# The diagonal 16x16 blocks of a delta-rule inverse, solved by forward substitution before the chunk loop instead of by doubling levels inside it

## What is computed

```
lower = where(strict, einsum('bhncd,bhnsd->bhncs', k_beta, k) * decay, 0.0)
sol = triangular_solve(lower, rhs, left_side=True, lower=True, unit_diagonal=True)
...
def step(state, inp):
    v_new = u_i - w_i @ state
    o_i = q_i @ state + a_i @ v_new
    state = state * cd_i + k_i^T @ v_new
```

## Time and profile before

| | |
|---|---|
| median of three runs | 1436.24 us |
| the profiled execution | 1442.7 us, of it 1441.0 us span |
| PE busy | 94% of the span |
| DVE, POOL, ACT busy | 53%, 51%, 38% |
| last projection round ends on PE | 402 us |
| first cum of the chunk stage (step 0) | 409.12 us |
| cum of step 1, of step 2 | 428.18, 456.75 us |
| step 8 begins on PE | 614.41 us |
| first matmul of the output projection | 648.90 us |

### The profile page before, as it was taken

One profiled execution on the slowest core, in us unless ns is written; L12 is line 12 of the kernel. 1 busy time (PEld: TensorE's weight loads), 2 busy tenths in 40 slices (PEclk: granted clock), 3 DMA queues, 4 the chain that ended last, 5 costly groups with the idle time before them and its releaser, 6 DMA issues.

```text
span 1441.0 us, 18144 instructions
## 1 busy us (share of the span) xinstructions
PE 1354.2 (94%) x6707; PEld 1134.1 (79%) x6707; DVE 769.5 (53%) x955; ACT 552.4 (38%) x749; POOL 731.1 (51%) x492
## 2 busy tenths in 40 slices
PE   3799999999968999989987999999999999999997
PEld 3468888888858999877865888888888887888886
DVE  2835344262446666625474656555655556457544
ACT  3234535262541221216264444444444444324321
POOL 4447758685742212222048665656565567444540
PEclk8699999999978999989998999999999999999999
DMA  8142424234250000110111333223333337543601
GB/s 328 41 132 60 131 73 116 74 86 123 66 131 2 1 0 0 58 59 0 30 30 29 89 88 82 70 74 82 88 88 88 88 113 283 181 137 119 232 32 59
DMA packets 137929, 128.42 MB, mean 89 GB/s; under 512 B 7423, under 2 KB 114188, under 8 KB 137868
## 3 DMA queue, kind: packets, MB, share of 16 engines
q1 hardware_dynamic: 137868, 127.60, 29.3%
HBM read 111.85 MB, written 15.74 MB: 89 GB/s over the span
## 4 chain that ended last, share of the span: by engine, by line
PE 69%; POOL 11%; issue 9%; DVE 6%; DMA 3%; ACT 1%; SPq 0%; POOLq 0%; DVEq 0%; ACTq 0%
PE ps L1957 18%; PE ps L1958 18%; PE ps L1959 18%; PE ps L2087 5%; POOL ada_raw L820 3%; PE ps L2106 3%; PE ps L2103 3%; POOL ada_raw L823 2%; POOL w_split L795 2%; DMA ada_first<-in_ada_w_dram 1%; POOL ada_raw L825 1%; DVE ada_first L1468 1%; POOL h_p L919 1%; DVE pm_b L1612 1%; DMA x_hi<-in_x_dram 1%
## 5 line engine op out<-in xcount | busy, mean ns | idle before, releaser
L1957 PE MATMUL ps<-h_p,w_units 128*128 128x512 f32 x616 | 241.9, 393 | 11.5 <-POOL h_p L919 10.0
L1958 PE MATMUL ps<-h_p,w_units 128*128 128x512 f32 x616 | 241.3, 392 | 0.0
L1959 PE MATMUL ps<-h_p,w_units 128*128 128x512 f32 x616 | 241.1, 391 | 0.0
L1957 PE MATMUL ps<-h,w_split 128*128 128x512 f32 x448 | 175.1, 391 | 0.0
L1959 PE MATMUL ps<-h,w_split 128*128 128x512 f32 x448 | 174.3, 389 | 0.0
L1958 PE MATMUL ps<-h,w_split 128*128 128x512 f32 x448 | 174.3, 389 | 0.0
L930 POOL TENSOR_TENSOR w_units<-f_units,w_units 128x512 fp32r<-128x512 f32 x88 | 112.8, 1292 | 113.9 <-ACT w_units L1283 47.6
L955 POOL TENSOR_TENSOR wd_split<-wd_raw,wd_split 128x1024 fp32r<-128x1024 f32 x44 | 109.7, 2500 | 109.5 <-ACT wd_split L1379 109.4
L1957 PEld LDWEIGHTS ps<-h_p,w_units 128*128 128x128 f32 x616 | 116.5, 189 | 37.0 <-issue 8.3
L1908 DVE TENSOR_TENSOR ad_split<-ad_raw,ad_split 128x512 fp32r<-128x512 f32 x40 | 98.5, 2477 | 78.3 <-ACT ad_split L1380 78.3
L1957 PE MATMUL ps<-wd_split,ad_split 128*128 128x512 f32 x352 | 137.1, 390 | 1.6 <-DVE ps L1866 1.3
(11 more groups left out here) (293 smaller groups left out, 2593.4 us busy)
## 6 DMA issues: line engine op xcount, KB each, us to landing
w_up_raw<-in_w_up_dram SPq DMA_DIRECT2D x44, 512.0 KB, 5.2
wd_raw<-in_w_down_dram SPq DMA_DIRECT2D x44, 512.0 KB, 4.2
ada_raw<-in_ada_w_dram SPq DMA_DIRECT2D x32, 512.0 KB, 4.1
w_raw<-in_w_in_dram SPq DMA_DIRECT2D x28, 512.0 KB, 5.4
act_dram<-cg SPq DMA_DIRECT2D x22, 512.0 KB, 3.3
ad_raw<-act_dram SPq DMA_DIRECT2D x44, 256.0 KB, 4.5
ada_first<-in_ada_w_dram SPq DMA_DIRECT2D x4, 2048.0 KB, 17.4
h_room<-in_w_out_dram SPq DMA_DIRECT2D x8, 512.0 KB, 13.4
```

What stands on the lines that cost most here:

```text
L1957: pe.matmul(dst, a_hi, b_hi, start=(first and n == 0), stop=False, skip_group_check=onto)
L1958: pe.matmul(dst, a_hi, b_lo, start=False, stop=False, skip_group_check=onto)
L1959: mm = pe.matmul(dst, a_lo, b_hi, start=False, stop=(last and n == len(pairs) - 1), skip_group_check=onto)
```

## The change

The inverses of all 16x16 diagonal blocks (4 heads x 8 chunks x 8 blocks = 256 blocks) are made once, before the chunk loop. A block lies in one partition, two blocks per partition (`kk_lanes`, `lower_lanes`, `inv_lanes`: 128 partitions x 2 x 16 x 16), and DVE runs forward substitution over the 15 columns, two small operations each. To get there, in the last projection round: PE makes the key products of all chunks between the two halves of the Z tile, ACT copies them to SBUF, SP moves the diagonal blocks to DRAM (32 DMAs) and back in the lane layout, and the gates go the same way (`gate_grid`, `gate_lanes`). The finished inverses go to DRAM and back as rows (`inv_rows`), first chunk 0 alone, then the other seven; `spread` on DVE multiplies them with a block mask into `um`. Levels 0 to 3 go out of the chunk stage: `level_a` is gone, `level_b` does levels 4, 5 and 6 only, and t1 transposes the spread `um`. POOL builds four masks instead of seven. Step 0 on DVE comes after the substitution in its list, and the loop's last projection round is written out separately.

```diff
-        A_LEVELS = [1]
-        B_LEVELS = list(range(2, LEVELS))
+        B_LEVELS = list(range(int(math.log2(SUB)), LEVELS))     # (beside level_mask)
@@ sync @@
+            sp.wait_ge(s.lane_step, L_TAKEN)
+            sp.dma_start(grid_dram.rearrange("a r n -> r a n"), gate_grid[0:NH * TT, :, :]).then_inc(s.diag_moved, 16)
+            sp.wait_ge(s.diag_moved, M_GRID)
+            sp.dma_start(gate_lanes[:, :, :, :], grid_dram.rearrange("a (m r) (b i) -> (r b) a m i", m=2, i=SUB)
+                         ).then_inc(s.diag_moved, 16)
+            sp.wait_ge(s.lane_step, L_DIFF)
+            for index, hd in enumerate(KK_ORDER):
+                sp.wait_ge(s.kk_copied, index + 1)
+                for b in range(NB):
+                    sp.dma_start(kk_dram[hd, :, b, :, :].rearrange("n r c -> r n c"),
+                                 kk_rows[hd][b * SUB:(b + 1) * SUB, :, b * SUB:(b + 1) * SUB]
+                                 ).then_inc(s.diag_moved, 16)
+            sp.wait_ge(s.diag_moved, M_KK_OUT)
+            sp.wait_ge(s.w_lo_done, NH * NPOS)
+            sp.dma_start(kk_lanes[:, :, :, :].rearrange("p m r c -> p m (r c)"),
+                         kk_dram.rearrange("(m h) n b r c -> (h n b) m (r c)", m=2)).then_inc(s.diag_moved, 16)
+            sp.wait_ge(s.lane_step, L_DONE)
+            sp.dma_start(inv_dram.rearrange("(m h) n b r c -> (h n b) m (r c)", m=2),
+                         inv_lanes[:, :, :, :].rearrange("p m r c -> p m (r c)")).then_inc(s.diag_moved, 16)
+            sp.wait_ge(s.diag_moved, M_INV_OUT)
+            inv_v = inv_dram.rearrange("h n b c i -> (b c) h n i")
+            sp.dma_start(inv_rows[:, :, 0, :], inv_v[:, :, 0, :]).then_inc(s.diag_moved, 16)
+            sp.wait_ge(s.diag_moved, M_INV_FIRST)
+            sp.wait_ge(s.dn_um, 1)
+            for hd in range(NH):
+                sp.dma_start(inv_rows[:, hd, 1:TT, :], inv_v[:, hd, 1:TT, :]).then_inc(s.diag_moved, 16)
@@ gpsimd, after the last round @@
+            pool.wait_ge(s.lane_step, L_DIFF)
+            pool.affine_select(out=lower_lanes[:, :, :, :], in_=lower_lanes[:, :, :, :], compare_op=ALU.is_ge,
+                               fill=-30000.0, base=-1, pattern=[[0, 2], [-1, SUB], [1, SUB]],
+                               channel_multiplier=0).then_inc(s.lane_step, 1)
...
+            pool.wait_ge(s.lane_step, L_DONE)
             dn_a(0, 0)
@@ scalar, proj_round(j, last) @@
                 inverse_norm(3 * j + 1, 1.0, None)
                 if not last:
                     proj_hi(AX, j + 1)
+                else:
+                    for index, hd in enumerate(KK_ORDER):
+                        act.wait_ge(s.kk_mm, index + 1)
+                        act.activation(kk_rows[hd][:, :, :].rearrange("p t n -> p (t n)"),
+                                       bank(KK_BANK[index], 2), ACT.Copy).then_inc(s.kk_copied, 1)
                 wait(s.silu_done, 3 * j + 2)
                 wait(s.k_norm, j + 1)
                 squares_of(q_t, j, 2)
+                if last:
+                    act.wait_ge(s.lane_step, L_MASKED)
+                    act.activation(lower_lanes[:, :, :, :], lower_lanes[:, :, :, :], ACT.Exp).then_inc(s.lane_step, 1)
@@ vector @@
+            def lane_gates():
+                dve.wait_ge(s.diag_moved, M_GATES)
+                dve.wait_ge(s.w_lo_done, NH * NPOS)
+                dve.tensor_tensor(lower_lanes, gates (by column), gates (by row), ALU.subtract)
+            def lane_beta():
+                (wait L_EXP; lower_lanes *= beta; wait tile_mm of Z; inv_lanes = identity)
+            def lane_inverse():
+                dve.wait_ge(s.diag_moved, M_KK_IN)
+                dve.wait_ge(s.lane_step, L_IDENT)
+                dve.tensor_tensor(lower_lanes[:, :, :, :], lower_lanes[:, :, :, :], kk_lanes[:, :, :, :],
+                                  ALU.mult).then_inc(s.lane_step, 1)
+                for j in range(SUB - 1):
+                    rows, cols = SUB - 1 - j, j + 1
+                    (wait) tmp = inv_lanes[:, :, 0:cols, j] * lower_lanes[:, :, j, j + 1:SUB]
+                    (wait) inv_lanes[:, :, 0:cols, j + 1:SUB] -= tmp
@@ vector, proj_round(j, last) @@
                 conv4(j, flat(q_t, j), bank(T_BANK[Q], 2), 0)
+                if last:
+                    lane_gates()
                 conv4(j, flat(v_t, j), bank(T_BANK[V], 2), 2)
                 dve.wait_ge(s.stat_rs, 3 * j + 2)
                 dve.tensor_tensor(flat(k_t, j), flat(k_t, j), sq[:, :], ALU.mult).then_inc(s.k_norm, 1)
                 squares_lo(q_t, j, 2)
+                if last:
+                    lane_beta()
+                    lane_inverse()
@@ vector, dn_step @@
-                    dve.tensor_tensor(pm_a[:, :, :], lt[:, slot, :, :],
-                                      level_mask[:, 0:1, :].to_broadcast([P, NH, P]), ALU.mult).then_inc(s.dn_a, 1)
-                    after(A_M0)
-                    wait_reuse(dve, s.dn_t_b, LB * (n - 1))
-                    wait_reuse(dve, s.dn_um_copied, n - 1)
-                    dve.tensor_tensor(um[:, slot, :, :], all_heads(ident), pm_a[:, :, :],
-                                      ALU.subtract).then_inc(s.dn_a, 1)
+                    if not (isinstance(n, int) and n == 0):
+                        spread(n, slot)          # one multiplication 128x512 into um; step 0: last in the step
@@ tensor @@
+            def kk_blocks(index):
+                hd = KK_ORDER[index]             # heads 0, 1, 3, 2; two pairs of banks in turn
+                pe.wait_ge(s.k_norm, hd + 1)
...
+                for n in range(TT):
+                    keys = k_t[:, hd, n * P:(n + 1) * P]
+                    mm = pe.matmul(dst[:, n, :], keys, keys, start=True, stop=True)
@@ tensor, dn_step @@
                 if a:
-                    pe.wait_ge(s.dn_a, n * A_STEPS + A_UM)
+                    pe.wait_ge(s.dn_um, n + 1)
+                    pe.wait_ge(s.dn_a, n * A_STEPS + A_KDIFF)
                     (t1)
-                for index in range(3, max(LB, 3 + LA)):
-                    (levels 5 and 6 of chunk n-1 and level 1 of chunk n: P, P, T, T, P, T)
```

More of the change, by code:

```diff
@@ L54, in build_program @@
     LEVELS = 7
+    SUB = 16
+    NB = P // SUB
     assert (L, D, AT, NH, DNW) == (1024, 1024, 4, 4, NH * P) and FT % 2 == 0
@@ L1187, in _ @@
             wait(s.dn_a, TT * A_STEPS)
-            wait(s.dn_al, TT * 3 * LA)
             wait(s.dn_kg, TT)
@@ L1560, in proj_round @@
+            def proj_round(j, last):
+                if last:
+                    dve.wait_ge(s.lane_step, L_GRID)
+                    dve.tensor_copy(gate_grid[0:NH * TT, :, :].rearrange("p a n -> p (a n)"),
+                                    bank(7)[0:NH * TT, 0:2 * P]).then_inc(s.lane_step, 1)
                 dve.wait_ge(s.ax_taken, j + 1)
@@ L1626, in level, with spread @@
                     dve.tensor_tensor(halves(um_done[:, :, :], lev)[:, 1, :, :], u, u_update,
[L1627 to L1633 removed]
+                                      ALU.subtract).then_inc(s.dn_b, 1)
+            def spread(n, slot):
+                dve.wait_ge(s.diag_moved, M_INV_FIRST if isinstance(n, int) and n == 0 else M_INV_REST)
+                wait_reuse(dve, s.dn_t_b, LB * (n - 1))
+                wait_reuse(dve, s.dn_um_copied, n - 1)
+                dve.tensor_tensor(um[:, slot, :, :].rearrange("p h (b i) -> p h b i", i=SUB),
+                                  inv_rows[:, :, ds(n, 1), :].to_broadcast([P, NH, NB, SUB]),
+                                  level_mask[:, LB:LB + 1, :].rearrange("p a (b i) -> p a b i", i=SUB)
+                                  .to_broadcast([P, NH, NB, SUB]), ALU.mult).then_inc(s.dn_um, 1)
             def dn_step(n, slot, a, b, c):
@@ L2034, in turn2, with gate_rows_turned, proj_tile @@
                 mm.then_inc(s.norm_turned, 1)
-            def proj_tile(pos, j, free):
+            def kk_blocks(index):
+                hd = KK_ORDER[index]
+                pe.wait_ge(s.k_norm, hd + 1)
+                if index < 2:
+                    pe.wait_ge(s.stat_ln, 3 * NH - 1)
+                    pe.wait_ge(s.mod_taken, NH - 1)
+                    pe.wait_ge(s.lane_step, L_TAKEN)
+                else:
+                    pe.wait_ge(s.kk_copied, index - 1)
+                dst = bank(KK_BANK[index], 2, P)
+                for n in range(TT):
+                    keys = k_t[:, hd, n * P:(n + 1) * P]
+                    mm = pe.matmul(dst[:, n, :], keys, keys, start=True, stop=True)
+                mm.then_inc(s.kk_mm, 1)
+            def gate_rows_turned():
+                pe.wait_ge(s.gates_ready, 1)
+                pe.matmul(bank(7)[0:NH * TT, 0:P], gate_by_head[:, 0, :], causal[:, :], start=True, stop=True)
+                pe.transpose(bank(7)[0:NH * TT, P:2 * P], gate_by_head[:, 1, :], ident[:, :]).then_inc(s.lane_step, 1)
+            def proj_tile(pos, j, free, between=None):
                 slot = W_SLOT[pos]
@@ L2041, in proj_tile @@
                 for half in range(2):
```

(14 more changed lines are left out.)

173 lines of the change are left out of this document (97 added, 76 removed).

## The result

The changed kernel takes 1390.72 us (median of 4 runs, 1388.62 to 1392.23) against 1436.61 us (1433.71 to 1437.6) on the same chip. The ratio is 0.9683, 95% interval [0.9664, 0.9702], so it is 45.9 us faster. The prediction said 1379, with a range from 1368 to 1400, and 1370 to 1389 for its forecast alone. The profiled execution of the changed kernel took 1392.23 us, of it 1390.5 span: 50.5 us less than before. The before execution that was profiled stood 6.1 us above its median, this one 1.5 above its own. These two offsets are the 4.6 us between the two differences.

What follows compares the result with a forecast made beforehand. PE, busy 94% of the span, was taken as the bound. Savings of 48.8 us (loop), 7.2 (step 1) and 14.0 (steps 8 and 9), less 13.0 before step 1, gave 57.0: median 1436.2 to 1379 us, range 1368 to 1400.

Steps and rivals of the forecast that it cites:

- PEclk 1.00 in the loop: In steps 2 to 7 PE's clock was to stay at 1.00, with steps of 17.8 us, or 18.8 with `ya_hi`.
- rival B: In the loop PE's clock falls to 0.50, making the kernel slower than before, at 1491 us; chance 0.05.
- (a): Before step 1: gate lanes there at about 396, V convolution moved by 5 us, head 3's keys at about 403.6.
- (b): Before step 1: two groups of key products on PE and ACT's copies of 1.0 us each, the last at 408.5.
- (c): Before step 1: SP issues eight DMAs per head, 0.35 us each, the last at 412.4; 64-byte packets landed at 417.
- (d): Before step 1: the load into the lanes takes 2.5 us, to 419.5.
- (e): Substitution on DVE: one operation of 0.7 us, then 30 at 0.28 us each, 8.4 us; done at 428.7.
- (f): After the substitution DVE does query norm (1.3), small ones (0.9), step 0 (7.2) and `spread` (0.7), to 438.8.
- (g): t1 at the low clock 1.12, tm 0.6, lt 0.63 us: cum of step 1 at 441.2 instead of 428.18.
- A: The small DMAs take the gain, with 64-byte packets at say 10 ns each: 1405 to 1415 us; chance 0.09.
- C: A step boundary costs 4 us instead of 1.7 to 2.7, or the tail stays: 1390 to 1398 us; chance 0.14.
- D: The state recurrence paces the loop, so the change doesn't shorten it: 1449 us; chance 0.01.

Runs made afterwards that it cites:

- the kernel with both copies moved: Changed kernel with `ya_hi` moved to mid-step and ACT's copy of the next gates into `lt` put ahead of the `tm` copy; 1376.68 us, ratio 0.9563.
- three edits: Changed kernel with `ya_hi` mid-step, `lt` copy ahead of `tm` copy, and DVE's query norm and its neighbours ahead of the substitution; 1372.59 us, ratio 0.9543.

## Why the prediction was right, and where its size was off

**The loop: the mechanism right, the clock not priced.** What was forecast of PE's list held: the level 4 to 6 order, the gap before cum and nowhere else of its size, ended by ACT's `lt`, 1.59 and 2.45 us. DVE has 77.42 / 6 = 12.9 us of work per step (predicted 12.3). The step that failed is "PEclk 1.00 in the loop", with the argument against rival B that step 8's other gaps were passed at 1.00 and that the 16 us between two gaps are gapless. By steps: steps 4 and 6 took 18.65 (18.8), but step 2 took 22.17 (18.8), steps 3 and 5 took 19.32 each (17.8), step 7 took 18.44 (16.85). These excesses are 3.4 + 1.5 + 1.5 + 1.6 us, less 0.3 for steps 4 and 6: 7.7, the whole miss of the loop, and every one goes with a gap of 2.45 us or 2.53. With the gaps into steps 3, 5 and 7 filled and the wait left in place these steps took 17.80, 17.79 and 16.89, so it is shown that the miss is the clock, and that filling the gaps keeps it up. What else decides whether a gap is followed by a fall stays open (see the last section). It was rival B, in part: the clock fell, but for 3.4 to 6.8 us at a time and not for the whole loop; each time it rose again while PE worked. The Trainium skill (TensorE: Matmul & The Clock Gate, "A second HAM failure mode: psum-queue depth-cycling") tells of a bf16 kernel in which short idles of PE between groups of matmuls came often enough to send the clock back and forth between its two levels. These runs agree, with one gap of 2.45 or 2.53 us at each fall in the changed kernel's loop; they add that gaps of 0.7 us did no harm in steps 3 to 8 of the kernel with both copies moved.

**Steps 8 and 9: the same term.** 22.02 us against 20.5. PE ran at 0.50 from about 583.7 to 587 in step 8, between sparse groups, as the kernel before did there. The prediction priced the tail at the full clock, and at the full clock it was right; the kernel with both copies moved had no fall there:

```profile
563.04:583.67 20.63, 17.54 (x145) 16.56 (x145) 8.62 (x16) 7.81 (x11) 13.03 (x6) 1.00 0.27 102
```

Four other kernels without a fall there (filled gaps, half packets, 16 DMAs, three edits) took 20.61 to 20.64 us.

**Step 1: better than forecast, by the clock too.** The forecast of 21.4 us took the clock's rise as late as before, where it was 0.52 over 428 to 440. In the changed kernel it rose 4.3 us after cum, and the step took 18.66. The kernel without the 30 operations had the late rise, 12 us after cum, and took 21.5. So the 2.7 us gained here are the time of the rise, not less work. That they came is luck: nothing in the forecast pointed to an earlier rise.

**The start: right within 1.5 us, by terms that partly cancelled.** Two traces of the changed kernel differ by as much (442.67 and 444.18). (a) The gate hops held DVE until 395.36 (396), but head 3's keys were ready at 401.7 (403.6): they moved by 3 us and not by 5. (b) ACT's last copy ended at 406.6 (408.5). (c) SP's issue was priced at 0.35 us each from a simple load and took 0.51; that is 5 us over 32 DMAs. With it SP was issuing without a pause, and the last issue came at 416.96 (412.4). The landing, for which 4.6 us were left, took 1.1, so the sum was met: 418.07 (417). The choice near the floor was right, but its reason was not: the packets cost next to nothing, and the issuing is the term. The Trainium skill's rule on transfers under 512 bytes (DMA: Bandwidth & Descriptors, the table at its head) therefore decides nothing here; half of the packets moved the lanes' load by 1 us. (d), (e): the lanes' load 2.6 us (2.5), the substitution 8.6 (8.4) at 0.19 to 0.29 us per operation. (f) The spread at 439.41 (438.1), with `scale2` at 1.24 us where 0.20 was usual. (g) 442.67 (441.2). The late transfers cost nothing, as taken: the other inverses were issued at 440.17, and step 1 did not wait for them.

**The rivals.** A did not come: the lanes' load went out at 418 and not at 442. C, a boundary of 4 us, did not come as a wait, though its time (1390 to 1398) is where the kernel landed. D is refuted by the loop's 41.1 us. The time of 1390.72 lies outside the 1370 to 1389 of the forecast itself; what held is the wider range. Rivals B and D together have 0.06, where the prediction wrote 0.05 for slower.

**The offset of the profile.** The prediction moved the saving of 57.0 us over to the median unchanged. Between the profiled executions the saving was 50.5, and between medians 45.9. Some 4.6 us of the difference to the forecast are this, and 6.5 are terms of the sum.

## What to carry to other kernels

When an edit takes work off an engine's list, look at what that work had covered, and price the gap that is left twice: as a wait, and as what it does to TensorE's clock behind it. Here the gaps of 2.45 and 2.53 us in the changed kernel's loop cost 1.5 to 3.4 us each on top of themselves, and moving two copies of 1.04 and 0.63 us out of the chain that PE waits for took the ratio from 0.968 to 0.956. Count DMAs before packets when one queue issues them all in a row, and before a second engine takes over a part of the issuing, look at what stands behind it in that engine's list: done at the wrong place it put the start off by 2.3 us, at the right one it moved it 3.1 us ahead (in the traces; in the times only the loss is seen). And an earlier start is not yet an earlier end: follow it through to the next step.

## What the runs showed of the hardware that was not expected

- The clock's fall depends on more than the length of one gap. The traces of the kernels here give these counts for the boundaries into steps 2 to 7. At gaps of 2.45 to 2.54 us (seven traces that have them as the changed kernel does) the clock fell in 27 of 28 cases. At 1.5 to 1.6 us it fell in 4 of 22: in three of six with `ya_hi` moved, in one of two with the filler, in none of 14 elsewhere. At 0.67 to 0.78 us it fell in 1 of 27, at the start of step 2 of the kernel with both copies moved, where PE had been busy only 1.16 and 1.55 us in the two windows of 2 us before. The one long gap that was passed at 1.00 is into step 3 of the kernel with 16 DMAs, which then took 17.79 us:

```profile
475.66 1.16 PE L2273 MATMUL ps<-causal,lt 128*128 128x128 f32 x8 [2.46 <-ACT lt L1195]
476.66 1.06 PE L2231 MATMUL ps<-tm,lt 128*128 128x128 f32 x8
```

- The rise after the sparse start came 3 to 4.5 us after cum of step 1 in nine traces (in the changed kernel 4.3 us, at 447.0), and 12 to 13 us after it in four: without the 30 operations (445.6), with the three edits (451.6) and in both kernels in which ACT issues eight DMAs (453.4 and 448.1). What decides between the two was not found. Step 1 took anything from 17.3 to 21.5 us, so an earlier start need not mean an earlier end.
- A DMA that stores 128 pieces of 64 bytes keeps SP's queue for 0.51 us and ACT's for 0.48 us, a simple one for 0.36 to 0.38 us.
